# Second attention of a two-block model: another order of TensorE's and ScalarE's work inside a step

## The chip, the cores and the metric

The kernel runs on one core of a Trainium2 chip. The metric is device time in microseconds (us), the median of several runs. Every figure below comes from the runs of the kernel before or from one profiled execution of it.

## What is computed

Two blocks follow each other on a sequence of 512 tokens with 1024 channels, all in float32. The first block has four layers (two conformer convolutions, one forgetting attention, one short convolution). The second block is one layer with two attention branches, a gate for each, an output projection and a feed-forward part. Cut to the part that the change touches, the reference is:

```python
h = rmsnorm(x, norm_mix)
q_a, k_a, v_a, q_i, k_i, w_i, q_b, kv_b, g_b, g_br = split(h @ w_in)
o_a = dsa_mixer(...)     # 8 heads, softmax over the best tokens of an index score
o_b = nsa_mixer(...)     # 8 heads in 2 groups: compressed, selected and window branch
gate_a, gate_b = split(g_br)
mix = sigmoid(gate_a) * (o_a @ w_branch_a) + sigmoid(gate_b) * (o_b @ w_branch_b)
x = x + mix @ w_out
```

Each attention branch is scores, plus a bias by distance and a mask, softmax, and weighing of the values.

## The kernel before

Every engine runs a program written out by hand, in its own order, and the engines meet only at semaphores. `wait_ge` stops an engine's whole queue until a named event has been counted; `then_inc` counts one. Large products are made of three passes (high part of the weight by high and by low part of the input, low part of the weight by the high part). ScalarE rounds a chunk of weights to its high part (`split_hi`, L373), GpSimd subtracts to get the low part (`split_lo`, L386), and SyncE loads the raw chunks.

The stretch in question is the loop over steps n = 0 to 13 in `second_tensor` (L2573 to 2583), with loops of the same index in `second_vector`, `second_scalar` and `second_gpsimd`. Two kinds of work share it. One is the 14 gate products: 24 matmuls of 128x512 each in bank 1, read out by VectorE into STAGE. The other is 12 pairs of heads (`PAIRS`), a pipeline three steps long. A pair has eight score blocks (i, e): i is the block of 128 queries, which sees (i+1)*128 keys, and e is the head of the pair. VectorE works on them in the order `BLOCKS` = (3,0), (3,1), (2,0), (2,1), then (1,0), (0,0), (1,1), (0,1).

- Scores of pair n+1 are made by TensorE at the end of step n (`pair_scores_tensor`, L2356). Block 3 lies in banks 4 and 5, block 1 in bank 7, blocks 2 and 0 in banks 2 and 3. All blocks but 3 wait until VectorE has read the last block, (0,1), of the pair before.
- VectorE in step n adds the bias and takes the maximum, block by block (`pair_scores_vector`, L2375; called the reading here, CUSTOM_DVE_ANT_0 in the trace, followed by an accumulator read). Four blocks are read, then come up to four steps of a top-k search (`best_vector`, MAX8 and MATCH_REPLACE8, which runs out about step 6), then the shares of pair n-1 (`pair_shares_vector`, L2409: a reciprocal, for n-1 < 8 a product with the gate, 4 or 8 TENSOR_SCALARs), the other four blocks, up to four more search steps, the gate's STAGE, and, where pair n-2 is the last of its output (pairs 1, 3, 5, 7 and 8 to 11), a COPY of bank 0, which waits for the weighing of pair n-2.
- ScalarE takes the exponentials of pair n (`pair_scores_scalar`).
- GpSimd multiplies the shares of e = 1 for pairs 0 to 5 in steps 1 to 6, and in steps 7 to 10 adds bias and mask for pair n+1 (`pair_fill_gpsimd`, L2393). In even steps it first makes a chunk's low part (`split_lo`), two TENSOR_TENSORs.
- TensorE in step n turns pair n-2 with transposes (`pair_turn_tensor`, L2436) in two groups, (3,0), (3,1), (2,0) and (2,1), (1,0), (1,1), in banks 6, 4 and 5. Since banks 4 and 5 also hold block 3 of the scores, (3,1) waits for the reading of (3,0) of pair n, and (2,0) for that of (3,1). ScalarE empties each turned group (`pair_turn_scalar`, L2453), and `pair_weigh_tensor` (L2460) multiplies with the values into bank 0 once all six are empty.

The order on TensorE in a step is: first turn group, half the gate product, second turn group, the other half, weighing of pair n-2, scores of pair n+1.

Of the kernel before, what the change touches and what calls it, by code (L numbers as in the profile page):

```python
# [149 lines left out]
def build_program(nc, x, vectors, b_f_bias, pe_k, w1_k, w2_k, pe_v, w1_v, w2_v, rel_bias, onehot, out,  # L150
# [3 lines left out]
    with ctx:  # L154
# [1889 lines left out]
        u_s, u_ttr, u_exp, u_sh, u_t, u_ev = (sig(n) for n in ("u_s", "u_ttr", "u_exp", "u_sh", "u_t", "u_ev"))  # L2044
# [93 lines left out]
        PAIRS = [Pair(n) for n in range(12)]  # L2138
# [217 lines left out]
        def pair_scores_tensor(pe, u):  # L2356
            if u.n < 8:
                pe.wait_ge(s_row, "qb", 3)
                pe.wait_ge(s_row, "kk", 1, 3)
            else:  # L2360
                pe.wait_ge(s_row, "qa", 3)
                pe.wait_ge(s_row, "ka")
            for i, e in ((3, 0), (3, 1), (1, 0), (2, 1), (2, 0), (0, 1), (0, 0), (1, 1)):
                if (i, e) == (1, 1):
                    pe.wait_ge(u_s, u.n, 1, 0)
                if u.n:
                    pe.wait_ge(u_ttr, u.n - 1, *((3, e) if i == 3 else (0, 1)))
                elif i == 3:
                    pe.wait_ge(s_cp, 2, e)
                else:  # L2370
                    pe.wait_ge(s_cev, 3 if i == 1 else e)
                pe.mm(u.scores(i, e), u.q[rows_of(e), i * P:(i + 1) * P], u.k[rows_of(e), 0:(i + 1) * P], True, True).then_inc(
                    u_s, u.n, i, e)
# [62 lines left out]
        def pair_turn_tensor(pe, u, i, e):  # L2436

            if (i, e) in TURN_GROUPS[1]:
                pe.wait_ge(u_ev, u.n, *TURN_GROUPS[0][TURN_GROUPS[1].index((i, e))])
            elif (i, e) != (3, 0):  # L2440
                pe.wait_ge(u_ttr, min(u.n + 2, 11), 3, TURN_GROUPS[0].index((i, e)) - 1)
            elif u.n:
                pe.wait_ge(u_ev, u.n - 1, 2, 1)
            else:
                pe.wait_ge(s_cev, 2)
            for m in (1, 0) if i == 1 else (i,):
                pe.wait_ge(u_shp if e and u.n < N_POOL_SHARES else u_sh, u.n, m, e)
                for k in range(m + 1):
                    c = P if i == 1 and m == 0 else 2 * P if i == 1 and k else k * P
                    op = pe.turn(turn_bank(i, e)[:, c:c + P], u.p[e][m][:, k * P:(k + 1) * P], ident[:, :])  # L2450
                op.then_inc(u_t, u.n, m, e)
# [38 lines left out]
        def second_tensor(pe):  # L2490
# [80 lines left out]
                    op.then_inc(s_g, "gate", n)  # L2571

            pair_scores_tensor(pe, PAIRS[0])  # L2573
            TURN_AT = {0: TURN_GROUPS[0], 4: TURN_GROUPS[1]}
            for n in range(14):
                for k in range(8):
                    for i, e in TURN_AT[k] if n >= 2 and k in TURN_AT else ():
                        pair_turn_tensor(pe, PAIRS[n - 2], i, e)
                    gate_part_tensor(n, (k,))
                if n >= 2:  # L2580
                    pair_weigh_tensor(pe, PAIRS[n - 2])
                if n < 11:
                    pair_scores_tensor(pe, PAIRS[n + 1])
            for n in range(14, 16):
                pe.wait_ge(u_ttr, 11, 0, n - 14)
                i, half, o = C_GATE + n // 2, n % 2, banks[n % 4][:, :]
# [9 lines left out]
            for quad in range(2):  # L2596
                for br in range(2):
                    i = C_BR + 2 * quad + br
                    for n in range(4):
                        half, cc, b = n // 2, (n % 2) * P, banks[4 * br + n][:, :]  # L2600
                        if quad:
                            pe.wait_ge(s_br_v, 0, br, n)
                        elif br == 0:
                            if n:
                                pe.wait_ge(s_gq, 12 + n)
                            else:
                                pe.wait_ge(u_o, 11)
                        elif n < 2:
                            pe.wait_ge(u_ttr, 11, 3, n)
                        elif n == 2:  # L2610
                            pe.wait_ge(u_ev, 11, 1, 1)
                        else:
                            pe.wait_ge(u_ttr, 11, 1, 1)
                        wait_low(pe, i, half)
                        for k in range(4):
                            s = br * 4 + k
                            pe.wait_ge(s_olv if s % 2 else s_olp, s)
                            wh, wl = halves(WH, i)[half][:, k, cc:cc + P], halves(WL, i)[half][:, k, cc:cc + P]
                            pe.mm(b, wh, hs(HH, s), k == 0, False)
                            pe.mm(b, wl, hs(HH, s), False, False)  # L2620
                            op = pe.mm(b, wh, hs(HL, s), False, k == 3)
                        op.then_inc(s_br, quad, br, n)
# [131 lines left out]
        def second_scalar(act):  # L2754
            split_hi(act, CS0 + 1)
            rms_scalar(act, 4)
            split_hi(act, CS0 + 2)
            rb_scalar(act, 4, banks[5], False)
            split_hi(act, CS0 + 3)
            split_hi(act, CS0 + 4)  # L2760
            for tb in range(NB):
                act.wait_ge(s_tokv, tb, 3)
            act.act(G, G, ACT.Sigmoid).then_inc(s_gate, "g")
            split_hi(act, C_KV + 1)
            index_scalar(act, 1, range(4))
            split_hi(act, C_KK + 1)
            index_scalar(act, 1, range(4, 8))
            compress_rest_scalar(act, 0, (0, HK[:, 0:31]), (1, HK[:, 32:63]))
            index_scalar(act, 2, range(4))
            split_hi(act, C_QB + 1)  # L2770
            index_scalar(act, 2, range(4, 8))
            compress_rest_scalar(act, 1, *((g, HV[:, g * 128 + r * 32:g * 128 + r * 32 + 31])
                                           for g in range(2) for r in range(4)))
            index_scalar(act, 3, range(4))
            split_hi(act, C_QB + 2)
            index_scalar(act, 3, range(4, 8))
            for j in range(2):
                split_hi(act, C_QA + j + 1)
                for i in range(NB):
                    if j:  # L2780
                        turned_scalar(act, i)
                    else:
                        compressed_scalar(act, i)
            for n in range(14):
                u, w = PAIRS[n] if n < 12 else None, PAIRS[n - 2] if n >= 2 else None
                if w:
                    for i in (3, 2, 1):
                        for e in range(2):
                            pair_turn_scalar(act, w, i, e)
                if n % 2 == 0:  # L2790
                    split_hi(act, C_GATE + n // 2 + 1)
                if u:
                    for i, e in BLOCKS:
                        pair_scores_scalar(act, u, i, e)
            for n in GATES_BACK[0]:
                act.wait_ge(s_gin[0], "gate", GATES_BACK[0][-1])
                act.act(GT[n], GT[n], ACT.Sigmoid).then_inc(s_gs, n)
            split_hi(act, C_BR)
            for s in range(8):
                act.wait_ge(s_g, *(("step", s) if s < 7 else ("gate", 15)))  # L2800
                act.wait_ge(u_o, 8 + s if s < 4 else 2 * (s - 4) + 1)
                act.act(hs(HH, s), (QA + QB)[s], ACT.Copy).then_inc(s_ohi, s)
            split_hi(act, C_BR + 1)
            for m in range(1, 4):
                for n in GATES_BACK[m]:
                    act.wait_ge(s_gin[m], "gate", GATES_BACK[m][-1])
                    act.act(GT[n], GT[n], ACT.Sigmoid).then_inc(s_gs, n)
                if m < 3:
                    split_hi(act, C_BR + 1 + m)
            for n in range(14, 16):  # L2810
                act.wait_ge(s_gq, n)
                act.act(GT[n], GT[n], ACT.Sigmoid).then_inc(s_gs, n)
            split_hi(act, C_BR + 4)
            for k in range(KD):
                act.wait_ge(s_mix, k)
                part_scalar(act, 4, k, MIX[k], lambda e, k: e.wait_ge(s_br, 1, k // 4, 3))
                if k == 3:
                    split_hi(act, FIRST_F - 3)
            for c in range(2, KD // 2 + 1):
                split_hi(act, FIRST_F - 4 + c)  # L2820
            for k in range(KD):
                scale_scalar(act, 5, vec["norm_mlp_2"], SQUARES[5], k)
# [319 lines left out]
```

## Time and profile before

| | us |
|---|---|
| median of 3 runs | 2487.79 (2487.3 to 2490.51) |
| profiled execution, its own time | 2488.68 |
| span of that execution | 2486.9 |
| TensorE busy (PE) | 2466.3, 99% |
| VectorE, ScalarE, GpSimd busy | 57%, 52%, 60% |
| the steps n = 2 to 13 in the span | 1872.20 to 2022.96 |

PE is TensorE's matmuls, DVE is VectorE, ACT ScalarE, POOL GpSimd. A line such as L64 is that of a helper that issues every matmul; L67 is the transposes, L112 the reading, L77 the shares, L73 sums, differences and products, L70 everything of ScalarE.

### The profile page before, as it was taken

The numbers are of one execution on the slowest core, as the hardware profiler recorded it, in microseconds if no ns is written. First come the engines' busy times: TensorE is split into PE (matmuls) and PEld (weight loads), VectorE is DVE, ScalarE is ACT, GpSimd is POOL, SyncE is SP. The second block draws the span as 40 slices with busy tenths as digits, with TensorE's granted clock in tenths as the row PEclk, the third lists the DMA queues.
The fourth block names the chain that finished last, engine by engine and source line by source line (L and its number), as shares of the span: only waits on it lengthen the run. The fifth ranks groups of instructions, "written<-read, shape, count | busy, mean of one in ns | idle before, by whom it ended". The sixth has DMA issues, their size and how long they took to land.

```text
span 2486.9 us, 31030 instructions
## 1 busy us (share of the span) xinstructions
PE 2466.3 (99%) x11629; PEld 2016.4 (81%) x11629; DVE 1417.5 (57%) x2423; ACT 1286.0 (52%) x1986; POOL 1500.9 (60%) x1017
## 2 busy tenths in 40 slices
PE   8999999999999999999999999999999999999998
PEld 6888887888888788888888888878877778888887
DVE  7999863155455524444441899986789642623102
ACT  7889744266567633222232788965345653423222
POOL 6999666453453555444455699956545556645663
PEclk9999999999999999999999999999999999999999
DMA  7888722355556323222222778862422242222221
GB/s 217 179 189 182 161 103 86 112 143 148 147 137 154 109 102 100 87 102 99 87 102 102 166 176 189 181 143 102 138 106 73 85 144 102 86 101 102 97 90 68
DMA packets 72193, 310.78 MB, mean 125 GB/s; under 512 B 8075, under 2 KB 8299, under 8 KB 58604
## 3 DMA queue, kind: packets, MB, share of 16 engines
q1 hardware_dynamic: 49164, 224.07, 26.7%
q0 software_dynamic: 22880, 84.73, 17.6%
q8 instruction: 93, 1.52, 0.2%
q14 instruction: 56, 0.46, 0.1%
HBM read 302.88 MB, written 5.89 MB: 124 GB/s over the span
## 4 chain that ended last, share of the span: by engine, by line
PE 85%; DVE 9%; POOL 2%; ACT 1%; issue 1%; DMA 1%; DVEq 0%; SPq 0%; POOLq 0%; ACTq 0%
PE ps L64 83%; DVE ps L81 6%; PE ps L67 2%; POOL AR L73 1%; POOL WL L73 1%; ACT AR L70 0%; POOL WL L115 0%; DVE ST L97 0%; DMA WL<-in_weights 0%; DVE AR L73 0%; DMA AR<-in_x 0%; DVE HL L73 0%; DVE AR L81 0%; ACT WH L70 0%; DVE AR L77 0%
## 5 line engine op out<-in xcount | busy, mean ns | idle before, releaser
L64 PE MATMUL ps<-HH,WH 128*128 128x512 f32 x3064 | 1204.4, 393 | 0.5 <-ACT WH L70 0.2
L64 PE MATMUL ps<-HL,WH 128*128 128x512 f32 x3064 | 1184.8, 389 | 0.0
L64 PE MATMUL ps<-HH,WL 128*128 128x512 f32 x3064 | 1089.8, 390 | 0.3 <-DMA WL<-in_weights 0.3
L73 POOL TENSOR_TENSOR WL<-WR,WH 128x1024 fp32r<-128x1024 f32 (+1 forms) x274 | 681.1, 2507 | 663.1 <-ACT WH L70 645.9
L64 PEld LDWEIGHTS ps<-HH,WH 128*128 128x128 f32 x3064 | 575.2, 188 | 129.8 <-ACT HH L70 4.7
L64 PEld LDWEIGHTS ps<-HH,WL 128*128 128x128 f32 x3064 | 574.7, 188 | 121.7 <-DMA WL<-in_weights 1.2
L64 PEld LDWEIGHTS ps<-HL,WH 128*128 128x128 f32 x3064 | 575.5, 188 | 118.1 <-issue 1.2
L70 ACT ACTIVATE WH<-WR 128x1024 fp32r<-128x1024 f32 (+1 forms) x403 | 408.2, 1046 | 441.6 <-PE ps L64 441.5
L81 DVE SCALAR_TENSOR_TENSOR ps<-AR,VEC,ps 128x512 f32<-128x512 f32 x652 | 448.9, 751 | 7.0 <-ACT ps L70 1.6
L73 POOL TENSOR_TENSOR AR<-AR 128x512 f32<-128x512 f32 x210 | 313.7, 1710 | 18.1 <-DVE HL L81 8.6
L70 ACT ACTIVATE AR<-ps 128x512 f32<-128x512 f32 (+3 forms) x263 | 130.6, 524 | 220.4 <-PE ps L64 140.9
L115 POOL DMA_DIRECT2D WL<-in_weights x129 | 145.2, 1125 | 132.8 <-ACT WL L70 132.8
L73 DVE TENSOR_TENSOR AR<-AR 128x512 f32<-128x512 f32 (+1 forms) x161 | 179.6, 1144 | 36.2 <-ACT AR L70 34.5
L70 ACT ACTIVATE AR<-AR,VEC 128x512 f32<-128x512 f32 x238 | 165.0, 731 | 49.3 <-DVE AR L73 31.9
L73 DVE TENSOR_TENSOR HL<-AR,HH 128x512 fp32r<-128x512 f32 x56 | 70.9, 1275 | 197.4 <-ACT HH L70 192.5
L73 DVE TENSOR_TENSOR AR<-ps,HT 128x512 f32<-128x512 f32 (+1 forms) x72 | 49.1, 687 | 221.8 <-PE ps L64 213.0
L64 PE MATMUL ps<-AR 128*128 128x128 f32 (+18 forms) x1146 | 159.6, 356 | 0.2 <-DVE AR L81 0.2
L64 PEld LDWEIGHTS ps<-AR 128*128 128x128 f32 (+5 forms) x1146 | 115.0, 174 | 42.0 <-issue 27.6
L70 ACT ACTIVATE AR<-AR 128x512 f32<-128x512 f32 (+3 forms) x72 | 40.9, 588 | 194.5 <-DVE AR L73 188.3
L73 POOL TENSOR_TENSOR AR<-AR,SQ 128x512 f32<-128x512 f32 x84 | 137.2, 1789 | 2.0
L70 ACT ACTIVATE WL<-WR 128x1024 fp32r<-128x1024 f32 x129 | 135.0, 1047 | 0.0
L73 DVE TENSOR_TENSOR AR<-AR,HT 128x512 f32<-128x512 f32 x48 | 71.3, 1485 | 97.5 <-ACT AR L70 97.0
(200 smaller groups left out, 2045.9 us busy)
## 6 DMA issues: line engine op xcount, KB each, us to landing
WR<-in_weights SPq DMA_DIRECT2D x105, 1024.0 KB, 4.8
WR<-in_weights SPq DMA_DIRECT2D x194, 512.0 KB, 4.8
WL<-in_weights POOLq DMA_DIRECT2D x129, 512.0 KB, 7.3
AR<-negc_rows POOLq DMA_DIRECT2D x16, 640.0 KB, 4.2
gate_rows<-WR SPq DMA_DIRECT2D x14, 256.0 KB, 2.9
AR<-gate_rows SPq DMA_DIRECT2D x14, 256.0 KB, 5.3
AR<-in_x SPq DMA_DIRECT2D x2, 1024.0 KB, 6.0
AR<-bias_by_distance POOLq DMA_DIRECT2D x1, 2048.0 KB, 8.6
```

The source lines that it names most:

```text
L64: return Op(None if self.e is None else self.e.matmul(o, l, r, start=first, stop=last, skip_group_check=True))
L67: return Op(None if self.e is None else self.e.transpose(o, i, identity))
L70: return Op(None if self.e is None else self.e.activation(o, i, f, **kw))
L73: return Op(None if self.e is None else self.e.tensor_tensor(o, a, b, op))
L81: return Op(None if self.e is None else self.e.scalar_tensor_tensor(o, a, s, b, op0, op1))
L115: return Op(None if self.e is None else self.e.dma_start(o, i, accum_op=ALU.add))
```

## The change

On TensorE, a step is now: first turn group, whole gate product, second turn group, scores of pair n+1 with block 3 last, weighing of pair n-2. Block 3 of the scores gets a wait for the emptying of block 1's turned tiles (banks 4 and 5). Weighing no longer stands before the scores. ScalarE empties the first turn group, splits the weight chunk (even steps), takes the first four exponentials, empties the second turn group, and takes the other four. Two waits after the loop name other events for the same banks. VectorE's, GpSimd's and SyncE's programs are unchanged.

```diff
-            for i, e in ((3, 0), (3, 1), (1, 0), (2, 1), (2, 0), (0, 1), (0, 0), (1, 1)):
+            for i, e in ((1, 0), (2, 1), (2, 0), (0, 1), (0, 0), (1, 1), (3, 0), (3, 1)):
                 if (i, e) == (1, 1):
                     pe.wait_ge(u_s, u.n, 1, 0)
+                if i == 3 and u.n >= 3:
+                    pe.wait_ge(u_ev, u.n - 3, 1, e)
...
-            TURN_AT = {0: TURN_GROUPS[0], 4: TURN_GROUPS[1]}
             for n in range(14):
-                for k in range(8):
-                    for i, e in TURN_AT[k] if n >= 2 and k in TURN_AT else ():
-                        pair_turn_tensor(pe, PAIRS[n - 2], i, e)
-                    gate_part_tensor(n, (k,))
+                for i, e in TURN_GROUPS[0] if n >= 2 else ():
+                    pair_turn_tensor(pe, PAIRS[n - 2], i, e)
+                gate_part_tensor(n, range(8))
+                for i, e in TURN_GROUPS[1] if n >= 2 else ():
+                    pair_turn_tensor(pe, PAIRS[n - 2], i, e)
+                if n < 11:
+                    pair_scores_tensor(pe, PAIRS[n + 1])
                 if n >= 2:
                     pair_weigh_tensor(pe, PAIRS[n - 2])
-                if n < 11:
-                    pair_scores_tensor(pe, PAIRS[n + 1])
...
-                            pe.wait_ge(u_ttr, 11, 3, n)
+                            pe.wait_ge(u_ev, 11, 1, n)
                         elif n == 2:
-                            pe.wait_ge(u_ev, 11, 1, 1)
+                            pe.wait_ge(u_ev, 11, 2, 1)
...
-                if w:
-                    for i in (3, 2, 1):
-                        for e in range(2):
-                            pair_turn_scalar(act, w, i, e)
+                for i, e in TURN_GROUPS[0] if w else ():
+                    pair_turn_scalar(act, w, i, e)
                 if n % 2 == 0:
                     split_hi(act, C_GATE + n // 2 + 1)
-                if u:
-                    for i, e in BLOCKS:
-                        pair_scores_scalar(act, u, i, e)
+                for i, e in BLOCKS[:4] if u else ():
+                    pair_scores_scalar(act, u, i, e)
+                for i, e in TURN_GROUPS[1] if w else ():
+                    pair_turn_scalar(act, w, i, e)
+                for i, e in BLOCKS[4:] if u else ():
+                    pair_scores_scalar(act, u, i, e)
```

## Rows read from the trace of the kernel before

**Rows 1.** The page, its first section: busy us (share) and instructions.

```profile
PE 2466.3 (99%) x11629; PEld 2016.4 (81%) x11629; DVE 1417.5 (57%) x2423; ACT 1286.0 (52%) x1986; POOL 1500.9 (60%) x1017
```

**Rows 2.** Windows, steps 4, 5, 8, 9, 11: length, busy PE, PEld, DVE, ACT, POOL, clock.

```profile
1898.95:1912.46 13.51, 13.51 (x90) 9.89 (x88) 11.22 (x36) 8.96 (x24) 6.71 (x4) 1.00 0.08 11
1912.46:1924.99 12.53, 12.53 (x86) 9.70 (x84) 12.26 (x37) 7.06 (x22) 7.62 (x8) 1.00 0.52 200
1951.07:1964.59 13.52, 13.52 (x90) 9.90 (x89) 5.69 (x25) 8.96 (x24) 6.70 (x5) 1.00 0.08 12
1964.59:1978.44 13.85, 12.98 (x86) 9.68 (x85) 9.12 (x30) 7.28 (x22) 10.35 (x12) 1.00 0.56 205
1990.95:2002.65 11.70, 10.63 (x71) 8.00 (x69) 7.23 (x26) 7.28 (x22) 4.76 (x6) 1.00 0.39 135
```

**Rows 3.** Timeline of TensorE: start, us, line, tiles, count, [idle before, releaser].

```profile
1869.84 2.43 PE L64 MATMUL ps<-AR 64*128 64x512 f32 x16
1906.79 5.75 PE L64 MATMUL ps<-AR 32*64 32x512 f32 x44
1912.46 0.66 PE L67 MATMUL ps<-ident,AR 128*128 128x128 f32 x4
...
1916.49 1.15 PE L67 MATMUL ps<-ident,AR 128*128 128x128 f32 x9
...
1965.55 0.66 PE L67 MATMUL ps<-ident,DG 128*128 128x128 f32 x4 [0.30 <-DVE SM L112]
1966.77 0.55 PE L67 MATMUL ps<-ident,SQ 128*128 128x128 f32 x3 [0.57 <-DVE SM L112]
...
2010.49 2.38 PE L64 MATMUL ps<-AR 128*64 128x128 f32 x24
```

**Rows 4.** Timeline of VectorE, steps 1 and 4.

```profile
1862.96 0.69 DVE L112 CUSTOM_DVE_ANT_0 SQ<-ps,AR 128x512 f32<-128x512 f32 x1 [0.36 <-PE ps L64]
...
1870.10 0.08 DVE L112 DVE_READ_ACCUMULATOR2_ANT SM<- 128x1 f32 x1
...
1897.08 0.68 DVE L84 COPY AR<-ps 128x512 f32<-128x512 f32 x1
1897.75 0.69 DVE L112 CUSTOM_DVE_ANT_0 SQ<-ps,AR 128x512 f32<-128x512 f32 x1
...
1903.15 0.17 DVE L73 TENSOR_TENSOR SM<-SM,AR 128x8 f32<-128x8 f32 x1
1903.36 1.28 DVE L77 TENSOR_SCALAR AR<-AR,SM 128x512 f32<-128x512 f32 x4
...
1905.45 0.29 DVE L112 CUSTOM_DVE_ANT_0 DG<-ps,AR 128x128 f32<-128x128 f32 x1
```

**Rows 5.** Timeline of ScalarE and GpSimd, before step 0 and in step 4.

```profile
1853.66 0.66 ACT L70 ACTIVATE AR<-ps 128x256 f32<-128x256 f32 x2 [5.25 <-PE ps L67]
...
1903.47 1.25 ACT L70 ACTIVATE AR<-ps 128x384 f32<-128x384 f32 x3 [2.36 <-PE ps L67]
1904.60 2.02 ACT L70 ACTIVATE WH<-WR 128x1024 fp32r<-128x1024 f32 x2
...
1905.75 4.73 POOL L73 TENSOR_TENSOR WL<-WR,WH 128x1024 fp32r<-128x1024 f32 x2 [10.24 <-ACT WH L70]
```

**Rows 6.** Timeline of VectorE and GpSimd where both read SBUF, and where not.

```profile
942.14 2.26 DVE L78 TENSOR_SCALAR SM<-SM 128x4 f32<-128x4 f32 x1
...
939.50 7.22 POOL L73 TENSOR_TENSOR WL<-WR,WH 128x1024 fp32r<-128x1024 f32 x3
...
1941.05 5.74 DVE L77 TENSOR_SCALAR AR<-AR,SM 128x384 f32<-128x384 f32 x6
...
1941.25 1.38 POOL L73 TENSOR_TENSOR AR<-AR,MR 128x512 f32<-128x512 f32 x1
...
1980.53 1.66 DVE L77 TENSOR_SCALAR AR<-AR,SM 128x384 f32<-128x384 f32 x6
```

**Rows 7.** Windows, TensorE's clock at a thin stretch of an earlier layer.

```profile
1368.60:1372.00 3.40, 3.40 (x11) 2.82 (x11) 1.69 (x7) 0.20 (x1) 0.00 (x0) 0.50 0.01 2
```

## The prediction

> **What bounds the kernel now.** I read the page first: TensorE is busy 99% of the span [rows 1]. So an edit helps only by removing TensorE's own time or its few idle moments, and it hurts by every microsecond that TensorE newly waits. Next I cut the loop into its steps with the windows [rows 2]. A step is 13.5 us where the weighed pair has the compressed branch (steps 4, 8) and 12.5 us otherwise (step 5). Step 9 is 13.85 us although its work is that of step 5, and step 11 is 11.70 us for 10.2 us of work: these are the only steps past 2 in which PE's busy time is short of the length. The timeline gives the parts [rows 3]: the second turn group takes 0.98 us, scores 2.36 (2.43 on the row, less the overlap with what follows), weighing 2.32 alone, 3.32 with the compressed branch (5.75 for both, less scores and overlap). The first turn group is 11 transposes against 9, so 1.2 us. What is left of the 12.53 us is the gate product, 5.7 us.
>
> Then VectorE. It is busy 11.2 and 12.3 us of steps 4 and 5 [rows 2], nearly as full as TensorE, until its search runs out. Its order is fixed. From its first reading of pair 4 at 1897.75 to the last at 1905.45 plus 0.3 it needs 8.0 us [rows 4]. TensorE must have that last reading before the next scores. Below, T is the moment when the first turn group of a step starts, and "reading" is VectorE's.
>
> **What the change removes.** (a) The second turn group no longer cuts the gate product in two. Every transpose and matmul stays, so only the switch between them can be saved. The step adds up to its parts with 0.1 to 0.2 us over [rows 2, 3], so a switch is worth from nothing to 0.15 us; I take 0.05, since the cut product shows no visible gap. Twelve steps: -0.6 us, at most -1.8. (b) In step 9 TensorE idles before (3,1) and (2,0) of the first turn group [rows 3], 1.3 us beyond the 12.53 of step 5 in all, and step 11 loses 1.5 us the same way [rows 2]. There the reading waits for GpSimd's bias and mask, which queue behind its two low-part operations, which in turn wait for ScalarE's split [rows 5]. ScalarE now splits before the second turn group instead of behind it, some 3 us earlier. Both losses go: -2.8 us. That is all there is to gain, at most 4.6 us, under the 0.2% (5.0 us) that a measurement of this kernel can tell from no change.
>
> **What it adds, part by part.**
>
> (c) The start. Scores of pair 0 now begin with block 1, which waits for ScalarE's last emptying before the loop, done at 1853.66 + 0.66 = 1854.32 [rows 5]; the scores began at about 1853.8. +0.6 us. With block 3 last, the first reading of a pair starts 2.36 - 0.85 = 1.5 us later in relation to the scores' start (0.85 us is an estimate for block 3, its 1024 of 2560 columns of 2.36 us, rounded down). In step 1 VectorE starts reading as soon as it may (it idles 0.36 us before 1862.96) and reads the last block at 1870.1 to 1870.2 [rows 4], while the next scores start at 1869.84 [rows 3]; block 3 in front covered the 0.3 us. Now the reading is 0.6 + 1.5 us later, and no block is free of it. TensorE waits about 2.0 us. Together +2.6.
>
> (d) The COPY. Where the weighed pair is the last of its output, VectorE copies bank 0 after the weighing and only then reads the next pair. Weighing stood before the scores, so COPY ran under them. Now weighing is last, at T the first turn group starts, and its (3,1) needs the first reading. COPY starts at T + 0.1 and takes 0.67 to the next start [rows 4], the reading of (3,0) with its accumulator read ends at T + 1.47, that of (3,1) at T + 2.1. TensorE, with three transposes left, starts the gate at T + 2.44 instead of T + 1.18: +1.26 us. Behind the waiting (3,1) stands everything of TensorE. This holds for steps 4, 6, 8, 10 and 11 (a last pair three steps back, and readings still to come). 5 x 1.26 = +6.3 us. In the other steps VectorE has read before T, behind 3.32 us of weighing: nothing.
>
> (e) The shares against the low parts. This is the largest term. In even steps ScalarE's split now starts about 0.45 us after the last emptying of the first group, at T + 3.15, GpSimd begins 1.15 us later [rows 5], and its two TENSOR_TENSORs run from T + 4.3 to T + 9.0. Before, they began 6.8 us after T (1905.75 against 1898.95), behind the shares. VectorE's shares in steps 4 and 6 now come at T + 0.78 + 5.4 to 5.6 [rows 4], in the middle of them. What that does is in the trace: six TENSOR_SCALARs took 5.74 us beside GpSimd's TENSOR_TENSORs of 1.38 and less, and 1.66 us with GpSimd quiet, and one of only 128x4 took 2.26 us beside the same low-part operation as here [rows 6]. So each such instruction of VectorE waits for one of GpSimd's, turn about. In step 4 the small product with the gate (two SBUF inputs) waits for the first low part, until T + 6.7, and the first share for the second, until T + 9.1; the four shares then run beside GpSimd's own shares and end at T + 11.1, and the last reading at T + 12.3. Scores could start at T + 2.44 + 5.7 + 0.98 = T + 9.1. TensorE waits 3.1 us. In step 6 the same; in step 2, without COPY but with the same collision, I take the same. In step 8 there is no search, the shares of eight blocks start at T + 3.5; three pass, two wait for a low part each, the rest ends at T + 11.5, the reading at 12.7: +3.6. In step 10 GpSimd goes straight on to bias and mask, so the last three shares wait for 1.3, 1.3 and 1.0 us more, and the reading ends at T + 15.2: +6.1. Sum 3 x 3.1 + 3.6 + 6.1 = +19.0 us. Nearest rows for the bounds: by the row of 1.66 us the term is 0; by that of 5.74 us it is 19, and a few us more if GpSimd's descriptors for the bias table join in. I take 19 since the very same low-part operation stands on the row of 2.26 us.
>
> The Trainium skill (SBUF — State Buffer, "SBUF: two separate sides") says that VectorE and GpSimd share a port pair as an exclusive lock held for the whole instruction. By that rule term (e) is the 19 us; were the ports shared by bandwidth it would be some 3 us. The trace agrees.
>
> (f) Weighing behind the turns. In steps 11 to 13 no scores stand between the second turn group and the weighing. Emptying starts 0.52 us into the group (1903.47 against 1902.95) and takes 1.25 [rows 5], so weighing can start at 1.87 us, where the transposes end at 0.98: 3 x 0.9 = +2.7 us. Up to step 10 scores of 2.36 us hide it; if ScalarE were late this cover would go too, but its exponentials end well before. Block 3's new wait (emptied at 1.4 us after the group's start) lies behind 0.98 + 1.5 us of other work: nothing.
>
> (g) The clock. TensorE's granted clock fell to half, 1.2 GHz, for 3.4 us at 1368.6 [rows 7], after some 3 us of products of one column. Work in such a stretch takes twice as long, so a fall costs up to 1.7 us. Stalls of 3 to 6 us are new in this loop; none of them to all five may cause it: 0 to +8.5, taken once, for the stall of 6 us: +1.7.
>
> GpSimd's and SyncE's queues: low parts and loads move earlier, and nobody waits for the chunks now. The tail after the loop has its chunks in time, so what is lost in the loop reaches the end in full.
>
> **Sum.** -0.6 - 2.8 + 2.6 + 6.3 + 19.0 + 2.7 + 1.7 = +28.9 us on the profiled execution's 2488.68: 2517.6 us. That execution stands 0.9 us over the median.
>
> **The rivals.** First, no collision: VectorE and GpSimd pass each other, because the split comes later than I think (the raw chunk, or ScalarE's exponentials in front). Then (e) and (g) vanish and 8.2 us remain: 2496.9. Against it: ScalarE has nothing between the first group and the split. In part, with one of the two low parts in the way, the time lies between, near 2507. Second, on the other side: the early reading decides. If VectorE had its COPY and readings done under the first turn group, and its whole chain of 8.0 us under the gate product of 5.7, only (a) and (b) remained: 2488.7 - 3.4 to 4.6 = 2484 to 2485. It decides from the point at which the COPY doesn't wait for the weighing; but it waits for it by name, so I hold it for unlikely. Third, the clock falls at every stall: 2524.4. A fourth is that the edit cancels out, gains of 4.6 against the small costs (c) and (f): 2489.
>
> **How the numbers follow.** Forecast (with or without the clock) 0.62, partial collision 0.14, no collision 0.12, cancelling 0.07, gains alone 0.05. The predicted time is that of the likeliest, 2517.6. The range takes in no collision and the clock's falls with 2.5 us on either side: 2494 to 2527; outside are the last two and what I haven't seen. Faster by over 0.2% would need more than all gains I can find: 0.03. Within 0.2%: 0.10. Slower: 0.87.
>
> **What would show it.** Windows by step: about 18 us for steps 4, 6 and 8, 20 for step 10, 12.5 for steps 3, 5, 7 and 9. In the timeline of TensorE an idle time of 0.4 to 1.1 us before (3,1), released by VectorE, in steps 4, 6, 8, 10 and 11, and one of about 3 us before the scores in even steps. TENSOR_SCALARs of VectorE of over 2 us beside GpSimd's WL<-WR,WH. A COPY that starts right at the end of weighing. The idle times of step 9 gone. The prediction is wrong if the shares in even steps take 1.3 us as before, or if the scores' waits are released by something else.

## The result

The changed kernel takes 2522.72 us (median of 4 runs, 2521.51 to 2527.16) against 2489.15 us (2487.3 to 2493.2) for the kernel before: a ratio of 1.0136, interval 1.0123 to 1.0148. That is 33.6 us slower; forecast were 28.9 us more, a time of 2517.6 us, and a range up to 2527. The profiled execution, the slowest of the four, has a span of 2525.0 us. One of the ten runs of the version "Both later" below took 9997.79 us, at a mean granted clock of 0.556, and is left out of its time.

The page answers [rows 1]: TensorE's share falls by a point.

```profile
PE 2474.7 (98%) x11629; PEld 2021.6 (80%) x11629; DVE 1446.7 (57%) x2423; ACT 1287.1 (51%) x1986; POOL 1502.2 (59%) x1017
```

The windows of the changed kernel, for steps 2 to 5 and 8 to 11, cut at the start of the first turn group as [rows 2] are (columns as there; the clock is the third number from the end):

```profile
1877.67:1894.39 16.72, 13.97 (x90) 9.82 (x89) 16.44 (x44) 9.21 (x24) 9.28 (x6) 1.00 0.26 94
1894.39:1906.86 12.47, 12.47 (x86) 9.65 (x84) 9.27 (x27) 7.05 (x22) 4.63 (x4) 1.00 0.06 22
1906.86:1925.83 18.97, 15.62 (x91) 10.96 (x89) 17.85 (x47) 9.21 (x24) 10.01 (x7) 0.91 0.35 114
1925.83:1938.30 12.47, 12.47 (x86) 9.65 (x84) 8.40 (x25) 7.04 (x22) 4.62 (x4) 1.00 0.10 39
...
1969.44:1994.07 24.63, 15.81 (x90) 11.09 (x89) 20.65 (x40) 9.21 (x24) 11.66 (x9) 0.86 0.26 96
1994.07:2006.54 12.47, 12.47 (x86) 9.65 (x84) 6.29 (x16) 7.05 (x22) 5.98 (x6) 1.00 0.06 21
2006.54:2027.03 20.49, 14.94 (x86) 10.87 (x85) 14.21 (x27) 9.21 (x24) 10.71 (x8) 0.83 0.35 116
2027.03:2039.21 12.18, 10.59 (x71) 8.30 (x69) 7.24 (x27) 7.18 (x22) 0.00 (x0) 1.00 0.08 30
```

Step 10 of the kernel before, which [rows 2] leave out:

```profile
1978.44:1990.95 12.51, 12.51 (x86) 9.70 (x84) 6.21 (x25) 8.96 (x24) 5.71 (x3) 1.00 0.17 57
```

The loss is in the even steps: step 4 took 13.51 us and takes 18.97, step 8 13.52 and 24.63, step 10 12.51 and 20.49. Steps 3 and 5 are what they were, 12.47 for 12.53, and step 9 has lost its idle time (13.85 to 12.47). VectorE's busy time over the whole span rises by 29.2 us, from 1417.5 to 1446.7, for the same 2423 instructions. (Its windows of single steps can't be compared one by one: the COPY and the first readings of step 4 now fall behind the start of the first turn group, 47 instructions in the window for 36.) TensorE's timeline names what it waits for:

```profile
1875.32 2.43 PE L64 MATMUL ps<-AR 64*128 64x256 f32 x16 [1.56 <-DVE SM L112]
...
1908.33 0.66 PE L67 MATMUL ps<-ident,WR 128*128 128x128 f32 x4 [0.81 <-DVE SM L112]
...
1918.46 7.43 PE L64 MATMUL ps<-AR 64*128 64x256 f32 x44 [2.53 <-DVE SM L112]
...
1986.55 7.59 PE L64 MATMUL ps<-AR 64*128 64x256 f32 x44 [8.01 <-DVE SM L112]
...
2020.36 6.74 PE L64 MATMUL ps<-AR 64*128 64x256 f32 x40 [4.73 <-DVE SM L112]
...
2036.89 2.38 PE L64 MATMUL ps<-AR 128*64 128x128 f32 x24 [0.78 <-ACT AR L70]
```

The rows are: the start (pair 2's scores), the turn of (3,1) behind COPY in step 4, the scores of steps 4, 8 and 10 behind VectorE's last reading, and the weighing of step 11 behind ScalarE's emptying. Scores with weighing last 7.43 us in step 4 where they lasted 5.75 [rows 3]: that is the clock, which was at half for 3.42 us of them (windows further below).

The loop itself, from its first scores to the end of the last weighing, took 203.57 us for 169.19. Ahead of it this execution took 3.8 us more (1857.60 for 1853.77). Of these 0.53 us is the new wait of the first scores; the rest lies in code that is the same in both: at 1781 us TensorE waited 2.37 us for VectorE in this execution and not in that of before. Behind the loop both took 463.9 us.

### The profile page after: what moved, and what is told of

Its sections match the earlier page's. It is cut to its first block, busy times and chain, and to the rows that moved or that the text cites. A ratio compares the mean times of both kernels' runs of the same rounds, so it can differ in the third digit from the quotient of the medians.

```text
span 2525.0 us, 31007 instructions
## 1 busy us (share of the span) xinstructions
PE 2474.7 (98%) x11629; PEld 2021.6 (80%) x11629; DVE 1446.7 (57%) x2423; ACT 1287.1 (51%) x1986; POOL 1502.2 (59%) x1017
## 4 chain that ended last, share of the span: by engine, by line
PE 79%; DVE 8%; POOL 7%; issue 3%; ACT 2%; DMA 1%; DVEq 0%; SPq 0%; POOLq 0%; ACTq 0%
PE ps L64 77%; POOL AR L73 5%; DVE ps L81 3%; PE ps L67 2%; POOL WL L115 1%; DVE AR L77 1%; DMA WL<-in_weights 1%; ACT AR L70 1%; POOL WL L73 1%; DVE AR L73 0%; ACT WH L70 0%; DVE HL L73 0%; DVE DG L73 0%; DMA AR<-in_x 0%; DVE SQ L73 0%
## 5 line engine op out<-in xcount | busy, mean ns | idle before, releaser
L64 PE MATMUL ps<-AR 128*128 128x128 f32 (+19 forms) x1146 | 166.6, 370 | 25.0 <-DVE SM L112 21.9
L64 PEld LDWEIGHTS ps<-AR 128*128 128x128 f32 (+6 forms) x1146 | 118.5, 182 | 64.4 <-issue 26.4
L70 ACT ACTIVATE AR<-AR 128x512 f32<-128x512 f32 (+3 forms) x72 | 40.9, 588 | 194.4 <-DVE AR L73 188.3
```

What stands on the lines that cost most here:

```text
L64: return Op(None if self.e is None else self.e.matmul(o, l, r, start=first, stop=last, skip_group_check=True))
L70: return Op(None if self.e is None else self.e.activation(o, i, f, **kw))
```

## The mechanism in the rows

VectorE and GpSimd of the changed kernel, step 4. The small product with the gate (0.59 us for 0.17) and the four shares (4.13 us for 1.28 [rows 4]) lie beside the two low parts.

```profile
1906.98 0.69 DVE L84 COPY AR<-ps 128x512 f32<-128x512 f32 x1 [3.04 <-PE ps L64]
...
1912.90 0.59 DVE L73 TENSOR_TENSOR SM<-SM,AR 128x8 f32<-128x8 f32 x1
1913.52 4.13 DVE L77 TENSOR_SCALAR AR<-AR,SM 128x512 f32<-128x512 f32 x4
...
1911.05 4.75 POOL L73 TENSOR_TENSOR WL<-WR,WH 128x1024 fp32r<-128x1024 f32 x2 [8.76 <-ACT WH L70]
```

COPY starts 0.12 us after the weighing's end at 1906.86, as forecast. The low parts start 4.19 us after it (T + 4.3 was forecast). The small product waits out the first of them, the first share the second (that share alone took 2.56 us).

## Experiments

Idle times below are TensorE's, read from its timeline. "Loop" is from the first scores to the end of the last weighing: 169.2 us before, 203.6 changed. Behind the loop all versions took 463.8 to 464.2 us in their profiles. Ahead of it, in code that no edit touched but for the 0.53 us wait of the first scores, they took 1853.1 to 1860.3 us, and the wait of 2.37 us stands in six of the eleven profiles. So medians of four runs carry some microseconds that no edit made, and the loop is the better measure.

**Split later.** ScalarE only:

```diff
-                if n % 2 == 0:
-                    split_hi(act, C_GATE + n // 2 + 1)
                 for i, e in BLOCKS[:4] if u else ():
                     pair_scores_scalar(act, u, i, e)
+                if n % 2 == 0:
+                    split_hi(act, C_GATE + n // 2 + 1)
```

> The changed kernel, with ScalarE's split of the weight chunk placed behind the first four exponentials instead of ahead of them; nothing else differs. Theory (GpSimd's two low parts block VectorE's shares): the low parts start near T + 6.8 us, so in steps 2, 8 and 10 the shares are over before them, no TENSOR_SCALAR of 2.5 us is left there, and the waits before the scores (2.6, 8.0, 4.7 us) and the two long stretches at half clock (about 4 us of loss) go. In steps 4 and 6, where COPY delays the shares to T + 6.4, one low part still catches them and up to 2.5 us of wait stay. Time about 2503 us (2499 to 2508). Rival (the scores wait because COPY and block 3 in the last place make VectorE late by themselves): within 3 us of the changed kernel, 2520 to 2525.

2510.74 us (2507.39 to 2512.91), ratio 1.0089 (1.0072 to 1.0106); loop 188.3. The waits before the scores of steps 2, 8 and 10 are gone, from 2.55, 8.01 and 4.73 us to nothing, though block 3 is last and COPY is where it was. The rival is out. In steps 4 and 6 I expected up to 2.5 us and 3.8 are left: two shares are caught now, one by each low part, so four shares take 5.49 us and not 4.13. Step 6 was also at half clock for 6.8 us, and its scores with weighing took 8.57 us for 5.75. Together these are some 4 us more than the 2503 us expected, which is what the profiled execution took, 2507.39. It was the fastest of the four; what the others add isn't shown.

```profile
1905.96 5.49 DVE L77 TENSOR_SCALAR AR<-AR,SM 128x512 f32<-128x512 f32 x4
...
1912.62 2.85 PE L64 MATMUL ps<-AR 64*128 64x256 f32 x14 [3.80 <-DVE SM L112]
```

**COPY later.** VectorE only:

```diff
+            def copy_out(u):
+                dve.wait_ge(u_w, u.n)
+                dve.copy(by_queries(u.out), by_queries(u.bank[:, :])[:, :, ::-1, :]).then_inc(u_o, u.n)
...
                     for i, e in BLOCKS[:4]:
                         pair_scores_vector(dve, PAIRS[n], i, e)
+                    if n >= 3 and PAIRS[n - 3].last:
+                        copy_out(PAIRS[n - 3])
...
-                if n >= 2 and PAIRS[n - 2].last:
-                    u = PAIRS[n - 2]
-                    dve.wait_ge(u_w, u.n)
-                    dve.copy(by_queries(u.out), by_queries(u.bank[:, :])[:, :, ::-1, :]).then_inc(u_o, u.n)
+                if n >= 11:
+                    copy_out(PAIRS[n - 2])
```

> The changed kernel, with VectorE's COPY of a last pair moved behind the first four readings of the next pair; the split stays early. Theory: the idle time of 0.8 us before the turn of (3,1) goes in all five steps (-6.0 us in all). In steps 8 and 10 the shares now come at about T + 1 to T + 4 and mostly miss the low parts, so those waits and slow stretches go too (about -16); in steps 2, 4 and 6 the collision stays, 2 to 3 us each. Time about 2500 us (2496 to 2506). Rival (COPY's delay is all there is): the waits before the scores vanish in steps 4 and 6 too, and with them their stretches at half clock, about 2492 us.

2508.88 us (2502.04 to 2509.86), ratio 1.0073 (1.0058 to 1.0088); loop 183.1. All five idle times of 0.81 us before (3,1) are gone, and so are the waits of steps 8 and 10; those of steps 2, 4 and 6 stay at 2.55, 2.75 and 2.74. COPY alone was not it. The loop gained 20.5 us of the 22 that I expected. The time lies over the forecast's range (2496 to 2506): the profiled execution took 5.7 us more ahead of the loop than that of before (1859.45 for 1853.77), the waits of 2.37 and 0.53 us among them. The fastest of the four runs took 2502.04 us.

**Both later.**

> The changed kernel with both edits: split behind the first four exponentials, COPY behind the first four readings. Theory: no share meets a low part except at its edge, no wait for COPY; left are the start (+2.1), weighing right behind the turns in steps 11 to 13 (+2.3), and the gain of bias and mask coming earlier (-2.8), so about 2490 us (2488 to 2493), the kernel before within 0.2%. Rival (the order on TensorE itself costs, for instance by switching between score and weighing tiles or by block 3 last): 2500 us or more, with waits or longer steps where no VectorE instruction is late.

2491.9 us (nine runs, 2490.42 to 2495.19), ratio 1.0008 (0.9998 to 1.0017); loop 170.8. TensorE's waits in the loop of this version (us in total, times, the longest):

```profile
PE ps L64 <- ACT AR L70: 2.9, 4, 0.8
PE ps L64 <- DVE SM L112: 1.6, 1, 1.6
PE ps L67 <- DVE SM L112: 0.5, 2, 0.3
```

In the changed kernel the rows released by VectorE's reading stood at 21.9 us and 4.3 us. The order on TensorE costs next to nothing by itself, 1.6 us in the loop: the 34 us, but for the start and the weighings of steps 11 to 13, came from where the split and COPY stood. No stretch of this loop is at half clock. That is the expected case.

**The table's DMA early.** GpSimd, step 8 only:

```diff
+                if n == 8:
+                    pool.wait_ge(u_ttr, n - 1, 0, 1)
+                    table_gpsimd(pool, n // 4, 0, n - 4, 4)
                 if n % 2 == 0:
                     split_lo(pool, C_GATE + n // 2 + 1)
...
-                if n in (4, 8):
+                if n == 4:
```

Why I tried it: in step 8 of the changed kernel one share of 128x128 took 5.18 us. VectorE's rows, then GpSimd's:

```profile
1976.41 2.47 DVE L77 TENSOR_SCALAR HT<-HT,SM 128x256 f32<-128x256 f32 x1
1978.80 5.18 DVE L77 TENSOR_SCALAR SQ<-SQ,SM 128x128 f32<-128x128 f32 x1
1983.90 0.82 DVE L77 TENSOR_SCALAR HT<-HT,SM 128x256 f32<-128x256 f32 x1
...
1973.62 5.10 POOL L73 TENSOR_TENSOR WL<-WR,WH 128x1024 fp32r<-128x1024 f32 x2 [6.99 <-ACT WH L70]
1978.67 0.80 POOL L118 DMA_DIRECT2D AR<-bias_by_distance  x1
1979.49 1.28 POOL L73 TENSOR_TENSOR AR<-AR,MR 128x512 f32<-128x512 f32 x1
1980.72 1.27 POOL L73 TENSOR_TENSOR VEC<-AR,MR 128x512 f32<-128x512 f32 x1
1981.94 3.36 POOL L73 TENSOR_TENSOR AR<-AR,MR 128x384 f32<-128x384 f32 x4
```

> The changed kernel, with GpSimd's issue of the second bias table's DMA (step 8) moved ahead of the chunk's low parts instead of behind them. It bears on the share of 128x128 that took 5.2 us in step 8 of the changed kernel, through the issue and four bias-and-mask operations. Theory (the DMA's issue breaks the turn-about, and VectorE loses its turn until much later): behind the low parts VectorE and GpSimd take turns again as in step 10, the wait before the scores of step 8 falls from 8.0 to about 4.5 to 5 us, and the time by 3 us, to about 2519.5. Rival (the share was starved for another reason, or the table lands later and something waits for it): no change, 2522.7, or slower.

With the issue moved, the same share takes 1.28 us and the wait before the scores 4.95 instead of 8.01:

```profile
1979.89 1.28 DVE L77 TENSOR_SCALAR SQ<-SQ,SM 128x128 f32<-128x128 f32 x1
...
1984.57 7.65 PE L64 MATMUL ps<-AR 64*128 64x256 f32 x44 [4.95 <-DVE SM L112]
```

So the wait does what the theory says, and the loop of this profile is 2.7 us shorter, 200.8. The time of the whole kernel didn't follow: 2523.11 us (2520.78 to 2527.15), ratio 1.0138 (1.0122 to 1.0153), no change against the changed kernel. I ran both again beside each other.

> The changed kernel itself, beside the next one on the same chip. Expected: 2522 to 2524 us, and the same waits before the scores as in its first profile (2.6, 2.5, 2.5, 8.0, 4.7 us); the stretches at half clock may fall on other steps.

> The version with the bias table's DMA ahead of the low parts, timed beside the changed kernel. Its wait in step 8 was 3 us shorter, its time was not. Theory one (the wait's gain is real and the first timing hid it): 3 us less than the changed kernel beside it, at most 1 us of which the clock takes back. Theory two (the clock takes it back: half-clock stretches come more often in this version, as the one in step 2 of its profile): equal within 1.5 us, and the profile again shows one stretch more inside the loop.

The changed kernel took 2523.91 us (2522.09 to 2526.55), with the same waits again, the other 2521.54 us (2518.14 to 2527.33), wait 4.93 us. The sign is that of theory one, but 2.4 us lie within the spread of either's runs, and the two timings together give about 1 us. The loops say more: 204.3 us in the changed kernel's second profile and 199.8 in the other, 4.5 less. Half-clock stretches in the loop were 23.9 us long in the first and 17.1 in the second, that is fewer, not more, with the table early; in the first pair 20.5 and 20.5. So in neither pair did the clock take the 3 us back. What hid them in the first pair's medians isn't shown beyond the spread ahead of the loop; how much the clock takes on average over many runs stays open.

**The split early, in the kernel before.** ScalarE only; TensorE's old order:

```diff
-                    for i in (3, 2, 1):
-                        for e in range(2):
-                            pair_turn_scalar(act, w, i, e)
+                    for i, e in TURN_GROUPS[0]:
+                        pair_turn_scalar(act, w, i, e)
                 if n % 2 == 0:
                     split_hi(act, C_GATE + n // 2 + 1)
+                if w:
+                    for i, e in TURN_GROUPS[1]:
+                        pair_turn_scalar(act, w, i, e)
```

> The kernel before, with one edit: ScalarE empties the first turn group, splits the weight chunk, and then empties the second group. TensorE's order is the old one. It brings the collision of GpSimd's low parts with VectorE's shares without COPY behind weighing. Theory (a collision makes VectorE 3 to 4 us late; what that costs depends on the slack to the next scores): in steps 2, 4 and 6 TENSOR_SCALARs of about 2.5 us appear, yet TensorE doesn't wait before the scores, since these stand behind weighing and begin with block 3. VectorE's lateness shows in the following step as waits before (3,1) of 1 to 2 us in steps 3, 5, 7. In steps 8 and 10 the shares are over before the low parts. Steps 9 and 11 lose their idle times (-2.8). In all 2489 to 2495 us. Rival (a collision costs its 3 us wherever it stands): 2500 us or more.

2491.31 us, ratio 1.0007 (0.9998 to 1.0017). The collision is there in full, four shares in 4.15 us in step 4, yet TensorE idles only 0.29, 0.41 and 0.56 us before (3,1) in steps 2, 3 and 5, less than I thought (the first stood before as well, 0.30):

```profile
1910.08 4.15 DVE L77 TENSOR_SCALAR AR<-AR,SM 128x512 f32<-128x512 f32 x4
...
1914.91 0.08 DVE L112 DVE_READ_ACCUMULATOR2_ANT SM<- 128x1 f32 x1
...
1912.27 5.75 PE L64 MATMUL ps<-AR 32*64 32x512 f32 x44
...
1919.16 0.66 PE L67 MATMUL ps<-ident,VEC 128*128 128x128 f32 x4 [0.56 <-DVE SM L112]
...
1965.47 5.18 DVE L77 TENSOR_SCALAR DG<-DG,SM 128x128 f32<-128x128 f32 x1
...
1971.82 1.74 PE L64 MATMUL ps<-AR 64*128 64x256 f32 x9 [2.05 <-DVE SM L112]
```

I was wrong on step 8: three shares were caught there too, the last one across the table's DMA, and 2.05 us of wait came out, with a stretch of 3.4 us at half clock behind it. VectorE had not fallen behind: its first share began 1.5 us after the start of the first turn group, as in the kernel before (1952.57 against 1951.07). But the eight shares took 2.5 us alone there, and the low parts now start 3.2 us after that point, not 6.8, so they catch the last three. My expectation had this sum wrong. The loop took 172.0 us, 2.8 more than before. The rival, 3 us for each collision, is out: in steps 2, 4 and 6 the same collisions cost 2.5 us each in the changed kernel and about 1 us in all here. The difference is the slack between VectorE's last reading and the scores that wait for it. In step 4 here the last reading is over at 1915.0, and the scores begin near 1915.6, behind 3.3 us of weighing; in the changed kernel TensorE stood ready 2.53 us too early. One thing more differs between the two, COPY behind the weighing, and "COPY later" shows that without it the collisions of steps 2, 4 and 6 still cost 2.55, 2.75 and 2.74 us.

**ScalarE's old order under TensorE's new one.**

> The changed kernel with ScalarE's order of the kernel before: both turn groups are emptied ahead of the split and of all exponentials. Theory: the split now waits for the second turn group, behind the whole gate product, so GpSimd's low parts start near T + 11.5 us and end in the next step. No share of VectorE meets them in the even steps (no wait before the scores there), but GpSimd's own shares and its bias and mask come too late: TensorE waits about 4 us in the first turn group of steps 3, 5 and 7 and 3 to 5 us in steps 9 and 11, and COPY's waits of 0.8 us stay. About 2517 us (2508 to 2525). Rival (it is TensorE's order that makes the waits before the scores, whatever ScalarE does): waits of 2.5 to 8 us before the scores in steps 2 to 10 as in the changed kernel.

2516.26 us (2512.14 to 2518.36), ratio 1.0104 (1.009 to 1.0117). No wait before the scores from step 2 on. In its place GpSimd is late, by its own shares in steps 3, 5 and 7 (1.8 us, where I said 4) and by its bias and mask in steps 9 and 11 (3.0 + 0.6 and 3.2 + 0.5 us):

```profile
PE ps L67 <- DVE SM L112: 10.8, 9, 3.2
PE ps L64 <- ACT AR L70: 2.9, 4, 0.8
PE ps L67 <- POOL VEC L77: 1.8, 1, 1.8
```

So the new order on TensorE needs the split neither where it is nor where it was, but between.

**Repaired.** Both edits of before, and two more:

```diff
-            for i, e in ((1, 0), (2, 1), (2, 0), (0, 1), (0, 0), (1, 1), (3, 0), (3, 1)):
+            blocks = ((1, 0), (2, 1), (2, 0), (0, 1), (0, 0), (1, 1))
+            for i, e in ((3, 0), (3, 1)) + blocks if u.n < 3 else blocks + ((3, 0), (3, 1)):
...
-                gate_part_tensor(n, range(8))
+                gate_part_tensor(n, range(4 if n >= 11 else 8))
...
+                if n >= 11:
+                    gate_part_tensor(n, range(4, 8))
```

> The version with split and COPY both later, and two repairs: block 3 of the scores comes first again for pairs 0 to 2, and in steps 11 to 13, where no scores stand before weighing, the second turn group is back in the middle of the gate product. Theory: the idle times at the start (0.5 and 1.6 us) and the three of 0.8 us before weighing go, 4.4 us in all, and nothing comes in their place, so 2 us less than the kernel before: about 2488 us, a ratio of 0.998 to 1.000. Rival (VectorE's lateness in the first steps moves on): a wait of 1 to 2 us before the scores or before (3,1) in steps 2 or 3, and the time of the version without the repairs, 2491 to 2493 us.

2488.44 us (11 runs), ratio 0.9996 (0.9987 to 1.0005) to the kernel before. The loop takes 166.8 us, 2.3 less than before, and one kind of wait is left in it:

```profile
PE ps L67 <- DVE SM L112: 0.6, 2, 0.3
```

In the loop the gain of 2 us is there as expected; in the time of the whole kernel it can't be told from none.

## Why the prediction was right, and where it was off

Direction, places and chain held. Term by term, against the rows of the changed kernel:

| term | forecast | found |
|---|---|---|
| (a) one visit instead of two | -0.6 | -0.06 in steps 3 and 5; if the same in all twelve, -0.7 |
| (b) bias and mask earlier | -2.8 | step 9 -1.3; in step 11 only COPY's wait is left before the turns, about -1.5 |
| (c) the start | +2.6 | waits of 0.53 and 1.56, +2.1 |
| (d) COPY in five steps | +6.3 | 0.81 idle and the gate 1.2 later each, +6.0 |
| (e) shares against low parts | +19.0 | 2.55, 2.53, 2.53, 8.01, 4.73: +20.4 |
| (f) weighing behind the turns | +2.7 | 3 x 0.78, +2.3 |
| (g) the clock | +1.7 | +6.9 |

The found terms make +34.2. Without the 0.53 us that lie ahead of the first scores they are 33.7, and the loop grew by 34.4; the 0.7 us between isn't placed.

Two terms were mis-sized. **The clock (g)** was taken once and came four times, in steps 4, 6, 8 and 10. The windows over two of these stretches (length, then busy times; the clock is the third number from the end):

```profile
1918.63:1922.05 3.42, 3.42 (x16) 2.51 (x16) 3.19 (x7) 0.95 (x5) 2.43 (x4) 0.50 0.50 176
...
1983.49:1990.32 6.83, 3.77 (x16) 2.79 (x16) 3.61 (x12) 1.86 (x8) 1.81 (x3) 0.50 0.42 165
```

With these stretches at 1.2 GHz in them the scores with weighing took 7.43, 7.14 and 7.59 us for 5.75, and 6.74 for 4.74 in step 10: 1.7, 1.4, 1.8 and 2.0 us, 6.9 in all. The wait of 2.55 us in step 2 brought no fall in this execution, one of the same length in step 4 did. **Step 8 of (e)** was put at 3.6 us and was 8.0. I had VectorE and GpSimd take turns throughout; across the DMA's issue they didn't (5.18 us for one share), which the early table took away, 3.1 us. My bounds named this ("a few us more if GpSimd's descriptors for the bias table join in"), my sum left it out without a reason. The rest of the gap is that the last three shares then meet bias and mask as in step 10. Against that, step 10 was put at 6.1 and was 4.7: its pattern was as forecast, but it ended 1.4 us sooner than I had added up. Steps 2, 4 and 6 were put at 3.1 and were 2.5.

Both misses point the same way, so the time came out 5 us above the forecast's. The bounds of (g), none to all five falls, and the rival of a fall at every stall, 2524.4, held it; that rival was nearer to what happened than the single fall in my sum. Part of the closeness is luck. The sum of (e) is off by only 1.4 us because step 8's 4.4 too little stood against 3.1 too much in the other four steps, and one of the four runs, 2527.16, lies at the edge of the range.

The rule of the Trainium skill on the shared port pair (SBUF — State Buffer, "SBUF: two separate sides"), that the loser blocks for the whole instruction, is what the rows show beside GpSimd's TENSOR_TENSORs, whatever the size: one of 128x4 took 2.26 us beside a low part [rows 6], and the share of 128x128 in the version with the early table 1.28 us beside one bias-and-mask operation of 1.3. There it was turn about, but for the DMA's issue. Beside GpSimd's own shares, TENSOR_SCALARs, the rows differ from that rule, and my "each such instruction of VectorE waits for one of GpSimd's" was too wide. Three shares of VectorE ran beside a single one of GpSimd's of 1.81 us (spans of GpSimd are rough in the profile), and the first of them took 0.84 us where such a share takes 0.41 with GpSimd quiet:

```profile
1915.77 1.81 POOL L77 TENSOR_SCALAR VEC<-VEC,SM 128x512 f32<-128x512 f32 x1
...
1916.01 0.84 DVE L77 TENSOR_SCALAR AR<-AR,SM 128x384 f32<-128x384 f32 x1
1916.77 0.89 DVE L77 TENSOR_SCALAR AR<-AR,SM 128x256 f32<-128x256 f32 x2
```

The sum hardly suffered from it: from the end of the second low part it gave the four shares 2.0 us in step 4, and they took 1.9. The "some 3 us" for a shared bandwidth was worked out from no row.

## What to carry to other kernels

Before moving a step, list what it feeds on the other engines, and lay those operations against the ones already there: here a split moved 3 us earlier on ScalarE, which had time for it, put GpSimd's two-input operations onto VectorE's shares. Here a collision cost only what exceeded the slack to the next waiter, and the edit to TensorE had just cut that slack. Then count what a stall of a few microseconds does to TensorE's clock, and count it for each stall.

## Of the hardware

An instruction of VectorE that was waiting beside GpSimd's work lost several turns, not one, when GpSimd issued a DMA in between: 5.18 us over the issue and four bias-and-mask operations, in the changed kernel (both profiles) and in the one with only the split early. With the issue moved away the same instruction took 1.28 us.

Waits of 2.53 us were followed by half clock for 3.4 us in steps 4 and 6 of the changed kernel, waits of 4.7 and 8.0 us by 6.8 us, part of it within the wait of 8.0. Which of the short ones bring a fall changes between executions of one kernel: steps 4 and 6 but not 2 in the first profile, steps 2 and 6 but not 4 in the second, all with waits of 2.5 us. The shortest wait in the loop with a half-clock stretch behind it was the 2.05 us of step 8 in the kernel with only the split early.
